# The opening of a two-layer decoder trunk: first projection slabs, gate slab and the gate's chain in another order

## The reference, cut to what matters

```python
y = xf * lax.rsqrt(jnp.mean(xf * xf, axis=-1, keepdims=True) + EPS) * g      # _rmsnorm
proj = h @ w_in                                                              # 1024 x 2312
qa, ka, va, fa, qb, kb, vb = _split(proj, EVEN_SIZES)                        # fa: 8 columns
log_f = jax.nn.log_sigmoid((fa + b_f).astype(jnp.float32))
F = jnp.cumsum(log_f, axis=1)
logits = q @ k.T * scale + F[t] - F[s]        # causal softmax, then values (attention A)
```

## Time and profile before

| what | us |
|---|---|
| median of 3 runs (1156.31 to 1157.19) | 1156.89 |
| the profiled execution | 1156.44 |
| its span in the trace | 1154.6 |
| TensorE busy | 1116.7 (97%) |
| VectorE busy | 880.0 (76%) |
| ScalarE busy | 614.8 (53%) |
| GpSimd busy | 387.9 (34%) |
| mean granted TensorE clock, of full speed | 0.997 |

### The profile page before, as it was taken

The page is one execution under the profiler, slowest core; times in us unless marked ns, Lnnn a source line. Parts: engine busy times, 40 slices in busy tenths (PEclk is TensorE's granted clock), DMA queues, the critical chain, the costliest instruction groups (busy, mean ns, idle before and its releaser), DMA issues.

```text
span 1154.6 us, 16567 instructions
## 1 busy us (share of the span) xinstructions
PE 1116.7 (97%) x6041; PEld 945.2 (82%) x6045; DVE 880.0 (76%) x1484; ACT 614.8 (53%) x1093; POOL 387.9 (34%) x313
## 2 busy tenths in 40 slices
PE   7999998999999999999999999999999999999996
PEld 5788887788989989989967778888878888888885
DVE  5877778678768678668768999656778677787686
ACT  6677677455344354344566377854454453443443
POOL 2444333551131141140175455435521221311400
PEclk9999999999999999999999999999999999999999
DMA  5242441441431521422222100214322424315212
GB/s 165 77 114 81 117 119 47 146 128 55 139 101 53 180 75 49 169 75 70 83 55 74 37 1 25 70 37 158 117 72 79 152 61 146 99 47 182 73 37 91
DMA packets 142226, 105.55 MB, mean 91 GB/s; under 512 B 9078, under 2 KB 122017, under 8 KB 142162
## 3 DMA queue, kind: packets, MB, share of 16 engines
q1 hardware_dynamic: 140892, 104.61, 29.6%
q10 hardware_dynamic: 1270, 0.13, 0.1%
HBM read 102.56 MB, written 6.35 MB: 94 GB/s over the span
## 4 chain that ended last, share of the span: by engine, by line
PE 75%; DVE 15%; ACT 5%; issue 3%; POOL 1%; DMA 1%; SPq 0%; ACTq 0%; DVEq 0%; POOLq 0%
PE bank L811 23%; PE bank L813 23%; PE bank L812 23%; DVE score L2488 2%; DVE best L2484 1%; DVE probT_l L2017 1%; ACT probs L1557 1%; PE bank L1021 1%; ACT ur L1311 1%; PE bank L1019 1%; PE bank L1031 1%; PE bank L1032 1%; POOL wl L1825 1%; DVE bank L2365 1%; DVE xhl L2088 1%
## 5 line engine op out<-in xcount | busy, mean ns | idle before, releaser
L1825 POOL TENSOR_TENSOR wl<-raw,wh 128x512 fp32r<-128x512 f32 x213 | 288.6, 1378 | 596.2 <-ACT wh L1311 560.0
L811 PE MATMUL bank<-ur,wh 128*128 128x512 f32 (+1 forms) x624 | 238.1, 382 | 1.1 <-POOL wl L1825 0.9
L813 PE MATMUL bank<-ur,wl 128*128 128x512 f32 (+1 forms) x624 | 236.3, 379 | 0.0
L812 PE MATMUL bank<-ur,wh 128*128 128x512 f32 x560 | 218.1, 390 | 0.0
L1311 ACT ACTIVATE wh<-raw 128x1024 fp32r<-128x1024 f32 x107 | 111.9, 1053 | 122.4 <-PE bank L813 120.5
L811 PEld LDWEIGHTS bank<-ur,wh 128*128 128x128 f32 x624 | 117.5, 188 | 24.5 <-issue 3.4
L813 PEld LDWEIGHTS bank<-ur,wl 128*128 128x128 f32 x624 | 117.5, 188 | 21.9
L812 PE MATMUL bank<-xhl,wh 128*128 128x512 f32 (+2 forms) x360 | 134.2, 373 | 0.0
L811 PE MATMUL bank<-xhl,wh 128*128 128x512 f32 (+1 forms) x296 | 120.9, 408 | 4.8 <-DVE xhl L2088 3.3
L811 PE MATMUL bank<-ur 128*128 128x256 f32 (+3 forms) x352 | 117.6, 334 | 6.7 <-ACT probs L1557 2.6
L812 PEld LDWEIGHTS bank<-ur,wh 128*128 128x128 f32 x560 | 105.2, 188 | 21.7 <-issue 0.5
(11 more groups left out here) (291 smaller groups left out, 2508.1 us busy)
## 6 DMA issues: line engine op xcount, KB each, us to landing
raw<-in_w_mlp SPq DMA_DIRECT2D x64, 512.0 KB, 4.0
raw<-in_w_in_e SPq DMA_DIRECT2D x18, 512.0 KB, 3.7
probs<-in_w_mlp SPq DMA_DIRECT2D x16, 512.0 KB, 4.6
rstd_qk<-in_w_mlp SPq DMA_DIRECT2D x16, 512.0 KB, 4.0
sq<-in_w_mlp SPq DMA_DIRECT2D x16, 512.0 KB, 4.8
raw<-in_w_in_o SPq DMA_DIRECT2D x10, 512.0 KB, 3.7
raw<-in_w_out_e SPq DMA_DIRECT2D x8, 512.0 KB, 3.8
score<-in_w_mlp SPq DMA_DIRECT2D x8, 512.0 KB, 6.1
```

Source lines behind the costliest of these rows:

```text
L811: mm(dst, lhs[0], rhs[0], start=start, stop=False, skip_group_check=not check)
L812: mm(dst, lhs[0], rhs[1], start=False, stop=False, skip_group_check=not check)
L813: return mm(dst, lhs[1], rhs[0], start=False, stop=stop, skip_group_check=not check)
L1825: return nc.gpsimd.tensor_tensor(dst, a, b, ALU.subtract)
```

## The change

- `opening_slab` replaces the first slab's loop: for each feature tile the two passes that need only `xh` come first, and the pass with `xl` of a tile comes one tile later.
- `gate_slab`: the 128 weight columns hold the high part of the gate's weights in 0 to 63 and the low part in 64 to 127, so that two passes (with `xh` and with `xl`) serve for three; one product more, low times low, comes with it. The spread comes after four tiles, not after the first.
- GpSimd subtracts only the eight true columns (`gate_rest`), and ScalarE repeats them (`split_gate_low`), between `xh` of tiles 6 and 7.
- `gate_taken` adds the two halves of the bank: one multiplication more, and the addition of the bias takes in the second half.
- VectorE makes the low parts of tiles 1 and 2 before the mean of squares, and all of them before the root is refined. ScalarE's root comes after tile 5.
- The load of the gate's weights goes ahead of the gains on ScalarE's queue.
- ScalarE rounds slab 3 before it places slab 0; VectorE starts the gate before it places slab 0, and finishes the gate (`fa`) before it places slab 2.

```diff
-                rows = HD if n == FA else P
-                slab(n, n % 2, pj(n)[0:rows, :], (xh, xl), (lambda k: pe.wait_ge(xg_lo, k + 1)) if n == 0 else None,
-                     width=rows, norm_part=norm_part, after=after)
+                slab(n, n % 2, pj(n)[:, :], (xh, xl), norm_part=norm_part, after=after)
...
+            def opening_slab():
+
+                dst = pj(0)[:, :]
+                pe.wait_ge(w_hi, 1)
+                pe.wait_ge(w_lo, 1)
+
+                def low_pass(k):
+                    pe.wait_ge(xg_lo, k + 1)
+                    return mm(dst, wh[:, 0, P * k:P * (k + 1)], xl[:, k, :], start=False, stop=k == KT - 1)
+
+                for k in range(KT):
+                    pe.wait_ge(xg_hi, k + 1)
+                    mm(dst, wh[:, 0, P * k:P * (k + 1)], xh[:, k, :], start=k == 0, stop=False)
+                    mm(dst, wl[:, 0, P * k:P * (k + 1)], xh[:, k, :], start=False, stop=False)
+                    if k:
+                        low_pass(k - 1)
+                low_pass(KT - 1).then_inc(slab_done, 1)
+
+            def gate_slab():
+
+                pe.wait_ge(w_hi, FA + 1)
+                pe.wait_ge(w_lo, FA + 1)
+                for k in range(KT):
+                    if k == 4:
+                        spread("mix_e")
+                    mm(pj(FA)[:, :], gate_w[:, k, :], xh[:, k, :], start=k == 0, stop=False)
+                    last = mm(pj(FA)[:, :], gate_w[:, k, :], xl[:, k, :], start=False, stop=k == KT - 1)
+                last.then_inc(slab_done, 1)
...
-            first_slab(0)
-            first_slab(1, lambda: spread("mix_e"), 0)
+            opening_slab()
+            gate_slab()
...
-                copy(repeated(wh[:, FA % 2, :]), gate_raw()).then_inc(w_hi, 1)
+                copy(gate_part(0), spread_columns(gate_raw)).then_inc(w_hi, 1)
+
+            def split_gate_low():
+
+                act.wait_ge(gate_low, 1)
+                copy(gate_part(1), spread_columns(gate_rest[:, :, :])).then_inc(w_lo, 1)
...
             act.dma_start(fixed[:, :], c_fixed[:, 0:P + N_GATE]).then_inc(fixed_loaded, 16)
+            act.dma_start(raw[:, FA % 2, 0:KT * NH].rearrange("p (k n) -> p k n", k=KT), weights_of(FA))\
+                .then_inc(raw_loaded[FA % 2], 16)
...
-            act.dma_start(raw[:, FA % 2, 0:KT * NH].rearrange("p (k n) -> p k n", k=KT), weights_of(FA))\
-                .then_inc(raw_loaded[FA % 2], 16)
...
-                if m == 4:
+                if m == 5:
                     root("mix_e")
+                if m == 6:
+                    split_gate_low()
...
+            split_slab(3)
             projected(0, EVEN[0][0], 0)
-            split_slab(3)
             gate_function(0)
...
-                    sub(repeated(wl[:, slot, :]), gate_raw(), repeated(wh[:, slot, :].bitcast(F32))).then_inc(w_lo, 1)
+                    sub(gate_rest[:, :, :], gate_raw, gate_w[:, :, 0:NH].bitcast(F32)).then_inc(gate_low, 1)
...
-                own.link(v.tensor_tensor(t0, pj(FA)[0:64, :], rstd[0:64, :], ALU.mult))
-                v.tensor_scalar(t0, t0, bfor[0:64, :], None, ALU.add).then_inc(slab_taken, 1)
+                v.tensor_tensor(t1, pj(FA)[HD:P, :], rstd[HD:P, :], ALU.mult)
+                own.link(v.tensor_tensor(t0, pj(FA)[0:HD, :], rstd[0:HD, :], ALU.mult))
+                v.scalar_tensor_tensor(t0, t0, bfor[0:64, :], t1, ALU.add, ALU.add).then_inc(slab_taken, 1)
...
+            for m in range(1, 3):
+                normed_lo("mix_e", m)
             mean_squares("mix_e", x_sums[:, :])
-            for m in range(1, 5):
+            for m in range(3, KT):
                 normed_lo("mix_e", m)
             refined_root("mix_e")
             diagonal("mix_e")
-            for m in range(5, KT):
-                normed_lo("mix_e", m)
...
+            gate_taken()
             projected(0, EVEN[0][0], 0)
-            gate_taken()
             gate_after_exp()
...
+            projected(None, "fa", FA)
             projected(1, EVEN[2][0], 2)
-            projected(None, "fa", FA)
```

More of the change, by code:

```diff
@@ L220, in trunk @@
         x_sums = sb("x_sums", [P, NQ])
-        spare = sb("spare", [P, 1])
+        spare = sb("spare", [P, 2])
+        gate_rest = sb("gate_rest", [P, KT, NH])
         at = [0]
@@ L385, in trunk @@
         causal_cut = sem("causal_cut")
+        gate_low = sem("gate_low")
         kr_lo = sem("kr_lo")
@@ L525, in head_slabs, with gate_part, spread_columns @@
             return (EVEN_AT[f"qa{t}"], EVEN_AT[f"va{t}"]) if attention(j) == "A" else (EVEN_AT[f"qb{t}"], EVEN_AT["vb"])
[L527 to L531, removed]
+        gate_w = wh[:, FA % 2, :].rearrange("p (k c) -> p k c", k=KT)
+        def gate_part(a):
+            return gate_w[:, :, HD * a:HD * (a + 1)].rearrange("p k (g c) -> p k g c", c=NH)
+        gate_raw = raw[:, FA % 2, 0:KT * NH].rearrange("p (k c) -> p k c", k=KT)
+        def spread_columns(w):
             return w.unsqueeze(2).to_broadcast([P, KT, HD // NH, NH])
@@ L1531, in load_exp @@
             def load_exp():
-                nc.scalar.activation(spare[:, :], ones[:, 0:1], ACT.Exp)
+                nc.scalar.activation(spare[:, 0:1], ones[:, 0:1], ACT.Exp)
             def probs_hi(s, parts=range(3)):
@@ L1691, in _ @@
             act.wait_ge(memsets_done, 1)
-            nc.scalar.activation(spare[:, :], ones[:, 0:1], ACT.Sqrt)
-            act.dma_start(raw[:, FA % 2, 0:KT * NH].rearrange("p (k n) -> p k n", k=KT), weights_of(FA))\
-                .then_inc(raw_loaded[FA % 2], 16)
+            nc.scalar.activation(spare[:, 0:1], ones[:, 0:1], ACT.Sqrt)
             square_row(0)
@@ L1716, in _ @@
             copy(causal[:, :], rstd_k[:, P:2 * P])
+            split_slab(3)
             projected(0, EVEN[0][0], 0)
-            split_slab(3)
             gate_function(0)
-            nc.scalar.activation(spare[:, :], ones[:, 0:1], ACT.Ln)
+            nc.scalar.activation(spare[:, 1:2], ones[:, 0:1], ACT.Ln)
             gate_function(1)
```

## The result

The median after is 1161.16 us over six runs (1157.66 to 1161.34), beside 1157.18 over six runs of the kernel before (1156.31 to 1157.55). The ratio is 1.0028, with an interval of 1.0017 to 1.0038: slower by about 3.2 us, where 1153.3 was predicted. The medians themselves differ by 4.0 us: four of the six runs lie between 1161.10 and 1161.34, the other two at 1157.66 and 1159.7, and the mean of the six is 1160.4. The profiled execution is the one of 1159.7 us, with a span of 1157.9, so its trace shows 3.3 us more than the span of before and not the whole of what the four longest runs lost.

The account below looks back on a forecast made before the run. TensorE was taken as the bound, 75% of the chain that ended last. Opening 1.66 + gate slab 1.82 + 0 + 0 = 3.5 us off 1156.4 gave 1152.9; as a median 1153.4, written 1153.3, range 1151.8 to 1155.3.

Parts of the forecast that it names:

- From slab 4 on: From slab 4 to the scores of head 1: slab 5 starts 4.4 us ahead, those scores 3.5 us ahead.
- The rival "slower": GpSimd beside the whole gate's chain makes operations 5 us longer in all; 1158.2 us; chance 0.04, including no gain.
- Opening: Start to slab 0's end: first pass at 13.15, slab 0 ends at 20.25 instead of 21.91, gaining 1.66 us.
- the rival that the clock doesn't fall: Opening: slab 0 then ends at 19.5, gain 4.2 us, median 1152.7; chance 0.17.
- one of the prediction's own signs of being wrong: Signs: slab 4 or slab 2 waits for `wl`, first pass after 14, or clock at 1.00 through the opening.
- The load moved ahead: Before slab 0: the gate's load ahead of the gains makes the third block of `x` land 0.4 us later.
- the gains come late: Opening: gains landing at 11.5 move the start by 1.5 us; gain 3.1 us, 1153.8; chance 0.07.
- Gate slab: Gate's slab after slab 0: 16 passes for 24, eight fewer at 0.227, saving 1.82 us.
- hidden: Slab 3's split ahead of `projected(0)`: ready at 29.2 us, wanted at 30.3, costing nothing.
- Gate's chain: Gate's chain up to slab 4's weights: 12.4 us, ready at 37.4, needed at 37.6; nothing lost.
- The absorbed lead: Rival at the scores of head 1: `take_slab(4)` comes later, gain falls to 1 to 2.5 us; chance 0.12.
- the stop before slab 5: Slab 5's 1.04 us wait for its low part ends and becomes a wait at the scores of head 1.

Follow-up runs that it names:

- k1: Kernel after with the old order of two VectorE calls, `projected(1)` ahead of `fa`; 1154.98 us, ratio 0.998 to before.
- k2: Kernel after, with GpSimd waiting after `prepare(0)` until VectorE has made qa0's low part; 1154.9 us, ratio 0.9976 to before.
- k3: Kernel before with nothing but the swap, `fa` ahead of `projected(1)`; 1163.12 us, ratio 1.0051 to before.
- k9: Kernel after, with GpSimd making slab 5's low part and then waiting for qa0's low part before slab 6's; 1156.41 us, ratio 0.9986.
- k12: Kernel after with GpSimd's low parts of slabs 5 and 6 as eight operations of 256 columns for four of 512; 1155.16 us, ratio 0.9979.
- k8: Kernel before with the new slab 0 and the opening's VectorE and ScalarE order alone, load not moved; 1156.31 us, ratio 0.9991.
- k6: k5 with the gate's load back behind the gains and the warming Sqrt on ScalarE's queue; 1153.02 us, ratio 0.9963 to before.
- k5: Kernel after with GpSimd waiting for qa0's and ka1's low parts, and `prepare(1)` ahead of slab 6; 1154.64 us, ratio 0.9971.
- k7: Kernel before with the two-pass gate slab, its weights and `gate_taken` alone; 1156.73 us, ratio 0.9998 to before.
- k11: k6 with thrown-away TensorE passes in the opening's three idle stretches (before slab 0, scores of head 0, slab 5); 1152.38 us, ratio 0.9951.
- k4: Kernel after with 22 thrown-away TensorE passes between slab 4 and the scores of head 0; 1157.76 us, ratio 1.001 to before.
- k10: Kernel after with `prepare(1)` moved between GpSimd's splits of slabs 5 and 6, no wait added; 1160.07 us, ratio 1.0015 to before.

## Why the prediction was wrong, point by point

**The step that failed** is in "From slab 4 on": "With `fa` ahead of `projected(1)` and the chain earlier, `prepare(0)` ends near 43.0". That time was right (GpSimd's operation at 42.16 ended at 43.41), but the step never costed what stands behind `fa`. `projected(1)` feeds the scores of head 0, and its two subtractions were moved onto GpSimd's five operations in a row. The sum has nothing for it. The cost was 5.4 us of blocking (6.07 for 0.69), so that TensorE stood 5.7 us where it stands 1.2 in k1 and 0.8 in k2, and then slow clock worth 2.0 to 3.4 us. k3 shows that the swap alone does it, k1 that taking only it away undoes it, k2 that keeping GpSimd off does too.

**The size of a contention** was the second error. I bounded a VectorE operation's loss at one GpSimd instruction, about 1.3 us, from the one pair 1.66 against 0.68 and from the Trainium skill, "SBUF — State Buffer", section "SBUF: two separate sides", by which the loser waits for the other's whole instruction. The trace after doesn't agree with that as a bound: one operation stood through `prepare(0)` and four halves. Elsewhere in the same trace, beside slab 3's split, VectorE lost only some 0.9 us (1.62 at 25.85, for 0.68 of the operation of the same kind at 34.11 in the earlier trace rows). That the two engines meet at a port is the account of the Trainium skill; what the runs show is that the block shrinks or goes when GpSimd's halves are held back (k9, k2) or cut in two (k12).

The trace of before held a sign of this. The sum took the two subtractions of ka1 over as "2.70" without asking why they take 2.70 us where qa0's take 1.39. One of them was beside the same four halves:

```profile
50.93 2.00 DVE L2017 TENSOR_TENSOR ur<-tbuf,ur 64x512 fp32r<-64x512 f32 x1 [2.90 <-ACT ur L1311]
...
47.38 5.00 POOL L1825 TENSOR_TENSOR wl<-raw,wh 128x512 fp32r<-128x512 f32 x4
```

It started in the third half and wasn't let in when the fourth began near 51.1, but ended at 52.93, again 0.55 us behind the last half (52.38). In k1 the same operation stood for 2.54 us and ended 0.55 us behind its run too.

**The rival "slower"** had the right mechanism with the wrong place and price: it looked at the gate's chain, where GpSimd has nothing to do, and at 1 us an operation.

**Opening: 1.66 us predicted, 2.22 measured** (19.69 for 21.91). The first pass came at 13.22 for 13.15. The sum had eight passes at the low clock in it, and none ran so: the rival that the clock doesn't fall was true in this execution, which is also one of the prediction's own signs of being wrong; the windows of every microsecond from 13 to 27 show 1.00, as here:

```profile
13.00:14.00 1.00, 0.78 (x3) 0.56 (x4) 0.77 (x2) 1.00 (x3) 0.00 (x0) 1.00 0.41 60
...
15.00:16.00 1.00, 1.00 (x5) 0.56 (x3) 0.96 (x4) 1.00 (x3) 0.32 (x1) 1.00 0.58 172
```

GpSimd's gate operation is down to 0.32 us from 1.86. What a term is worth by itself is another matter: with the opening alone k8 gains 0.5 us by the medians, at the edge of what can be told from nothing.

**The load moved ahead: 0.4 us predicted.** The third block of `x` took 7.0 us to land for 6.7, and with the load moved back the first pass starts 0.35 us earlier (k6 against k5, one execution each). Both agree with the term. That the gains come late was false: the gate's load landed 6.3 us after its issue, not 9.9, and the copy of the gains' transpose starts at 10.98 and holds nobody.

**Gate slab: 1.82 us predicted, 1.85 measured** (24.22 - 19.69 = 4.53, for 6.38). By itself it brings nothing (k7): slabs 3 and 4 then wait 1.5 us for low parts. In the combined kernel, where slab 3's split is moved ahead, there is no wait before slab 3, as "hidden" in my sum has it. Which of the moved orders does this wasn't tested alone.

**Gate's chain: slab 4's low part ready at 37.4 predicted, 36.88 measured**, for a slab that starts at 37.02. The slack of 0.2 us was 0.14. Slab 4 ended at 43.24, predicted 43.7.

**The absorbed lead.** That the scores of head 1 hang on ka1's low part holds in part: k2 and k1, with GpSimd beside that pair (2.74 and 3.24 us), come to 55.41 and 54.89, k5 and k6 with 1.39 us to 53.50 and 51.58. The clock moves these marks too, so the share of each isn't separated. And the stop before slab 5, 1.04 us before, which the sum let end, stayed in all of these (1.02 us in k1 and k2, 1.05 in k5, 1.03 in k6).

**The last 0.9 us.** At the first instruction after the 2.59 us idle stretch in layer 1 the kernel after is 2.4 us behind (672.32 for 669.91), and its span 3.3 behind. The stretch behind it ran at 0.74 in the kernel after and at 1.00 in the one before:

```profile
670.00:675.00 5.00, 2.68 (x12) 2.31 (x13) 4.93 (x14) 3.84 (x12) 1.10 (x1) 0.74 0.01 2
```

The change touches nothing there. In the profiled executions of nine of the twelve variants the clock averaged 0.83 to 0.91 between 660 and 680 us, and in k6, k7 and k11 1.00, as before. So it isn't bound to the opening's order, and what decides it stays open. The runs of before alone spread over 3 us.

## What to carry to other kernels

Before two calls are swapped on one engine, lay the moved instructions on the timeline of the engine that will run beside them, and look for a run without gaps: here a VectorE operation with both operands in SBUF waited through a whole run of GpSimd, 5.4 us, and not through one instruction only. A wait in TensorE's path can cost twice, as here: once as idle time and once as slow clock behind it; passes that are thrown away gave the second part back (k4). And a term that saves TensorE's time can be given back at the low parts, copies and waits behind it if they aren't moved with it: alone, the gate's slab was worth nothing and the opening about 0.5 us by the medians; together, with the right order and GpSimd kept off (k6), they were worth 3.8 us by the medians.

## What the runs showed of the hardware that I had not expected

- A 64x512 subtraction of VectorE took 6.07 us beside `prepare(0)` and four back-to-back GpSimd operations of 1.2 us, 3.63 us beside one and two, 5.61 us in k10, 0.7 us beside `prepare(0)` alone (k2), and 1.17 us when the same work came as eight operations of half the length. Each long block ended 0.55 to 0.6 us behind the end of a GpSimd operation. What decides when VectorE gets its turn stays open: neither a count nor a time fits all of them.
- The granted clock fell to 0.50 between 47 and 48 us, within the idle stretch that began at 43.24, and the 5.3 us behind that stretch ran at 0.50. It also fell after much shorter stops in some executions (k5, 0.81 and 1.05 us) and not in others with the same stops (k6, 0.77 and 1.03 us). Why isn't shown.
- In the kernel after the clock stayed at 1.00 through 1.26 us of idle time before the first pass, where the kernel before lost 3 us of it at 0.50 behind 2.16 us.
